# Paged sample attention: one key step per page instead of one per half page

## The chip, the core and the metric

The kernel runs on one core of one Trainium2 chip. The metric is the device time of one execution in microseconds (us). The engines of the core are TensorE (PE, whose weight loads are listed as PEld), VectorE (DVE), ScalarE (ACT), GpSimdE (POOL) and SyncE (SP, which issues nearly all DMA transfers).

## What is computed

The program is one inference step of a decoder layer for 256 prompt tokens and for 8 sequences ("batches") of 4 sample tokens each. The change concerns the attention of the sample tokens to their paged key cache of 1024 positions, 8 pages of 128 positions, 8 heads of width 128:

```python
past_k = cache_k[l][page_table].reshape(DB, past, MOBA_HEADS, MOBA_DH)
...
gate = jnp.einsum('bthd,bnhd->bthn', qq.astype(jnp.float32), kbar)   # kbar: mean key of a block of 256
...
s = (jnp.einsum('bthd,bthnkd->bthnk', qq, kg).astype(jnp.float32)
     - slopes[None, None, :, None, None] * dist.astype(jnp.float32))
p = jax.nn.softmax(s.reshape(B, qb, H, -1), axis=-1).reshape(s.shape)
return jnp.einsum('bthnk,bthnkd->bthd', p.astype(vg.dtype), vg).astype(q.dtype)
```

Each query keeps its three best past blocks of four and its own block. The kernel computes the scores of all eight pages and masks the worst block afterwards, so the keys of every page are read, transposed and multiplied with the queries.

## The kernel before, in words

Every engine has its own hand-written instruction stream. Within a stream the order is that of the program, and semaphores join the streams. Most of the kernel is large products of weights with 288 tokens: ACT rounds a weight tile into a high part (`hi`), DVE makes the remainder (`lo`), and `tile` on PE multiplies both (lines 1699, 1700, 1703). The sample attention is woven into one stage of that work: `d_batch` runs eight times, once for each batch, on each of PE, ACT and DVE.

On PE a batch of `d_batch` goes through these pieces in order:

- `tile(p_gm, b, 0, 0, 0)`, a gate tile of 48 products.
- `rows_t(b)`: two transposes that carry the previous batch's output rows into bank 5, after ACT copied them out of bank 4 (`rows_out`, semaphore `d_va`). DVE takes the result out of bank 5 in `rows_in` (line 1348) and counts `d_h`.
- The key steps, 16 half pages and a loop of 17 turns. In turn n PE makes four transposes of keys (line 1717, through `tr`) into bank 2 + n % 2, and then the four scores of the half page before (line 1713, through `one`). A score is a matmul with a stationary operand of 32 columns, and the four of a half page write to four different groups of 32 partitions of bank 6 or 7. The trace shows two records for each score.
- Between transposes and scores, a half page is copied from its bank to the buffer `KTb[n % 2]`: the even ones by ACT (line 831, called from `d_batch`, semaphore `d_kta`), the odd ones by DVE (line 1359, semaphore `d_ktd`). A copy waits for the transposes (`d_tr`) and for the scores that read the buffer last (`d_ss`).
- After the steps come the wait for `d_h`, eight scores against the batch's own keys into bank 5, and then `d_sc`, which starts the softmax on DVE.
- A second gate tile and a half tile run on PE while DVE and ACT make the softmax. Then follow the transposes of the probabilities (wait for `d_pn`), another half tile, and the products with the value pages (`PT`, line 1713).

DVE runs `rows_in` after its third key copy, while PE goes on.

The pages come in through four rings of two pages. SP issues the key pages of the next batch as the value products release the rings (`kv_read`), and the value pages as the key scores release them. The order of SP's queue is written out by hand: the next gate weights, eight value pages, the next projection weights (`pm_load`), eight key pages (line 493 issues pages, line 437 weights).

`d_P`, the score and probability rows, and `PT`, their transposes, share memory. They are used only after the key steps of a batch.

Of the kernel before, what the change touches and what calls it, by code (L numbers as in the profile page):

```python
# [14 lines left out]
P = 128  # L15
# [3 lines left out]
NS = NB * TS  # L19
NT = TP + NS  # L20
H, DH = 8, 128
# [16 lines left out]
GROUPS = P // NS  # L38
# [127 lines left out]
def build(nc, a, o):  # L166
# [24 lines left out]
    with ctx:  # L191
# [3 lines left out]
        def at(name, shape, offset, dt=F32):  # L195
            return nc.alloc_sbuf_tensor_at(name, shape, dt, offset=offset)

        def put(name, shape, dt=F32):
            off = top[0]
            n = 4 * int(np.prod(shape[1:]))  # L200
            top[0] = off + (n + 31) // 32 * 32
            assert top[0] <= nc.sbuf_usable_end, (name, top[0])
            return at(name, shape, off, dt)
# [83 lines left out]
        dmn, dmx, dsum = put("d_min", [P, 1]), put("d_max", [P, 1]), put("d_sum", [P, 1])  # L287
        dp_at = top[0]
        DP = put("d_P", [P, PAST + NS])
        PT = at("d_PT", [P, PAGES, P], dp_at)  # L290
        PTown = put("d_PT_own", [NS, P])
        hrow = put("d_hrow", [P, 2 * P])
# [123 lines left out]
        def ring(r):  # L416

            return raw[1 + r // 2][:, (r % 2) * 2 * H * DH:(r % 2 + 1) * 2 * H * DH]
# [214 lines left out]
        def _(act):  # L633
# [184 lines left out]
            mo_body(4, False, True)  # L818


            def k_copies(kts, tr_sem, ss_sem, mine, base, i, parity, copy, between=None):

                for n in range(parity, 16, 2):
                    act.wait_ge(tr_sem, i * 16 + (base + n + 1))
                    act.wait_ge(ss_sem, i * 16 + (base + n + 1))
                    copy(kts[n % 2][:], B[2 + n % 4][:].rearrange("p (h c) -> p h c", c=P)).then_inc(mine, 1)
                    if n == 4 and between:
                        between()

            def a_copy(dst, src):  # L830
                return nc.scalar.activation(dst, src, ACT.Copy)  # L831
# [14 lines left out]
            def d_batch(b, first):  # L846
                for j in range(2):
                    hi(p_gm, b, 0, j, src256(p_gm.slot(0), j))
                if not first:
                    rows_out(b)  # L850
                for n in range(0, 16, 2):
                    act.wait_ge(d_tr, b * 16 + (n + 1))
                    act.wait_ge(d_ss, b * 16 + (n + 1))
                    a_copy(KTb[0][:], B[2][:].rearrange("p (h c) -> p h c", c=P)).then_inc(d_kta, 1)
                gate_evac(p_gm, b, 0)
                pm_hi(b, 0)
                act.wait_ge(d_sm, b + 1)
                nc.scalar.activation(DP[:], DP[:], ACT.Exp, bias=dmx[:], accum_out=dsum[:]).then_inc(d_p, 1)
                gate_evac(p_gm, b, 1)
                pm_hi(b, 1)  # L860
                act.wait_ge(d_ptr, b + 1)
                a_copy(PTown[:], B[4][0:NS, 2 * P:3 * P])
                for q in range(2):
                    last = a_copy(PT[:, 4 * q:4 * q + 4, :], B[2 + q][:].rearrange("p (n c) -> p n c", c=P))
                last.then_inc(d_ptc, 1)
# [84 lines left out]
                    last = nc.scalar.activation(xP[:, h, r, :], xP[:, h, r, :], ACT.Exp, bias=xmx[:, h, r:r + 1], accum_out=xsm[:, h, r:r + 1])  # L950
            last.then_inc(c_step, 1)

            k_copies(xKT, d_tr, d_ss, d_kta, 128, 0, 0, a_copy)
            act.wait_ge(c_step, c_ptr)
            for h in range(XH):
                last = a_copy(xPT[:, h, :], B[2 + h][:])
# [84 lines left out]
        def _(dve):  # L1041
# [281 lines left out]
            dc.end(4)  # L1323


            def k_copies(kts, tr_sem, ss_sem, mine, base, i):
                for n in range(1, 16, 2):
                    dve.wait_ge(tr_sem, i * 16 + (base + n + 1))
                    dve.wait_ge(ss_sem, i * 16 + (base + n + 1))
                    nc.vector.tensor_copy(kts[1][:], B[2 + n % 4][:].rearrange("p (h c) -> p h c", c=P)).then_inc(mine, 1)  # L1330

            def gate_sig(ph, i, t, n):
# [13 lines left out]
            def rows_in(b):  # L1346
                dve.wait_ge(d_ht, b)
                nc.vector.tensor_copy(hsd[:, :, ds(b * TS - TS, TS)],
                                      B[5][:, 0:H * (NS + TS)].rearrange("p (h c) -> p h c", c=NS + TS)[:, :, 0:TS]).then_inc(d_h, 1)

            def d_batch(b, first):
                nc.vector.tensor_copy(qpad[:].rearrange("p (h c) -> p h c", c=NS + TS)[:, :, 0:TS],
                                      qs[:, :, ds(b * TS, TS)]).then_inc(d_q, 1)
                for j in range(2):
                    lo(p_gm, b, 0, j, src256(p_gm.slot(0), j))
                for n in range(1, 16, 2):
                    dve.wait_ge(d_tr, b * 16 + (n + 1))
                    dve.wait_ge(d_ss, b * 16 + (n + 1))
                    nc.vector.tensor_copy(KTb[1][:], B[3][:].rearrange("p (h c) -> p h c", c=P)).then_inc(d_ktd, 1)  # L1359
                    if n == 5 and not first:  # L1360
                        rows_in(b)

                dve.wait_ge(d_sc, b + 1)
                for q in range(2):
                    dc.run(nc.vector.reduce_sum(gs[:, 2 * q:2 * q + 2], B[6 + q][:].rearrange("p (n c) -> p n c", c=256), AX))
                dc.sync()
                dc.run(nc.vector.tensor_reduce(dmn[:], gs[:], AX, ALU.min))
                dc.sync()
                dc.run(nc.vector.scalar_tensor_tensor(geq[:], gs[:], dmn[:], K["rank"], ALU.is_equal, ALU.mult))
                dc.sync()  # L1370
                dc.run(nc.vector.reduce_max(dmx[:], geq[:], AX))
                dc.sync()
                dc.run(nc.vector.tensor_scalar(pen[:], geq[:], dmx[:], NEG, ALU.is_equal, ALU.mult))
                dc.sync()
                for n in range(BLOCKS):
                    dc.run(nc.vector.scalar_tensor_tensor(DP[:, n * 256:(n + 1) * 256], B[6 + n // 2][:, (n % 2) * 256:(n % 2) * 256 + 256],
                                                          pen[:, n:n + 1], dtab[:, n * 256:(n + 1) * 256], ALU.add, ALU.add))
                dc.run(nc.vector.tensor_tensor(DP[:, PAST:], B[5][:, 256:256 + NS], dtab[:, ds(b * -TS + (PAST + OWN), NS)], ALU.add))
                dc.sync()
                dc.run(nc.vector.reduce_max(dmx[:], DP[:], AX))  # L1380
                dc.sync()
                nc.vector.tensor_scalar(dmx[:], dmx[:], -1.0, None, ALU.mult).then_inc(d_sm, 1)
                pm_lo(b, 0)
                dve.wait_ge(d_p, b + 1)
                dc.run(nc.vector.reciprocal(dsum[:], dsum[:]))
                dc.sync()
                nc.vector.tensor_scalar(DP[:], DP[:], dsum[:], None, ALU.mult).then_inc(d_pn, 1)
                pm_lo(b, 1)
                gate_sig(p_gm, b, 0, 2)
                for j in range(2):  # L1390
                    dve.wait_ge(gemm_done, p_gm.conv(b, 3 + j))
                    nc.vector.tensor_tensor(U[:, ds(b * 2 + j, 1), :], G[p_gm.bank(2 + j)][:, 0:NT].unsqueeze(1), sg[:, j:j + 1, :],
                                            ALU.mult).then_inc(evac_done[p_gm.bank(2 + j)], 1)
# [127 lines left out]
            dc.sync()  # L1521
            nc.vector.tensor_scalar(xmx[:], xmx[:], -1.0, None, ALU.mult).then_inc(c_step, 1)

            k_copies(xKT, d_tr, d_ss, d_ktd, 128, 0)

            dve.wait_ge(c_step, c_p)
            dc.run(nc.vector.reciprocal(xsm[:], xsm[:]))
# [157 lines left out]
        def _(pe):  # L1685
# [29 lines left out]
            def tr(out, src):  # L1715
                n = src.shape[0]
                return nc.tensor.transpose(out, src, ident[0:n, 0:n])  # L1717
# [233 lines left out]
            def d_batch(b, first):  # L1951
# [2 lines left out]
                    rows_t(b)  # L1954
                pe.wait_ge(d_q, b + 1)

                for n in range(17):
                    if n < 16:
                        r, page = n // 4, n // 2 % 2
                        if n % 4 == 0:  # L1960
                            pe.wait_ge(kv_landed[r], b * 64 + 32)
                        for m in range(4):
                            c = page * H * DH + (4 * (n % 2) + m) * DH
                            last = tr(B[2 + n % 2][:, m * P:(m + 1) * P], ring(r)[:, c:c + DH])
                        last.then_inc(d_tr, 1)
                    if n:
                        pe.wait_ge((d_kta, d_ktd)[(n - 1) % 2], b * 8 + ((n - 1) // 2 + 1))
                        page = (n - 1) // 2
                        for m in range(4):
                            h = 4 * ((n - 1) % 2) + m  # L1970
                            last = one(B[6 + page // 4][m * NS:(m + 1) * NS, (page % 4) * P:(page % 4 + 1) * P],
                                       qpad[:, h * NS:(h + 1) * NS], KTb[(n - 1) % 2][:, m, :], start=h < GROUPS, stop=h >= GROUPS)
                            if m == 0 and n % 4 == 0:
                                last.then_inc(kv_read[n // 4 - 1], 1)
                        last.then_inc(d_ss, 1)
                pe.wait_ge(d_h, b + 1)
                for h in range(H):
# [239 lines left out]
```

## Time and profile before

| what | us |
|---|---|
| three timed runs | 2280.73, 2289.93, 2290.65 |
| their median | 2289.93 |
| the profiled execution's own time | 2281.03 |
| its span in the trace | 2279.5 |
| PE busy in the span | 2130.7 |
| DVE busy | 1206.3 |
| ACT busy | 797.3 |

PE is busy 93% of the span. Matmul records overlap each other, because matmuls are pipelined, so the start of a group of records minus the start of the next tells more than their summed durations. Times in the rows are microseconds from the start of the span, and the columns are explained where a view first appears.

### The profile page before, as it was taken

The numbers are of one execution on the slowest core, as the hardware profiler recorded it, in microseconds if no ns is written. First come the engines' busy times: TensorE is split into PE (matmuls) and PEld (weight loads), VectorE is DVE, ScalarE is ACT, GpSimd is POOL, SyncE is SP. The second block draws the span as 40 slices with busy tenths as digits, with TensorE's granted clock in tenths as the row PEclk, the third lists the DMA queues.
The fourth block names the chain that finished last, engine by engine and source line by source line (L and its number), as shares of the span: only waits on it lengthen the run. The fifth ranks groups of instructions, "written<-read, shape, count | busy, mean of one in ns | idle before, by whom it ended". The sixth has DMA issues, their size and how long they took to land.

```text
span 2279.5 us, 40609 instructions
## 1 busy us (share of the span) xinstructions
PE 2130.7 (93%) x16438; PEld 2009.2 (88%) x16438; DVE 1206.3 (53%) x1424; ACT 797.3 (35%) x1010; POOL 63.5 (3%) x85
## 2 busy tenths in 40 slices
PE   4999997998999999898899877999999999999997
PEld 4989896998778788888899756999999999999997
DVE  4354465343556465656446535666564456666444
ACT  3333332343333333323234333333333333333333
POOL 0011011010000000000000000000000000000000
PEclk7999997999999999999899988999999999999999
DMA  7145434454686876554444451454545555454543
GB/s 244 47 151 175 150 105 140 132 175 145 216 315 244 306 273 219 176 163 147 164 143 157 162 185 37 148 175 157 168 134 173 158 180 183 147 176 144 171 154 115
DMA packets 305491, 384.78 MB, mean 169 GB/s; under 512 B 6146, under 2 KB 278690, under 8 KB 304626
## 3 DMA queue, kind: packets, MB, share of 16 engines
q1 hardware_dynamic: 300530, 365.72, 48.9%
q0 software_dynamic: 4896, 18.13, 2.5%
q8 instruction: 49, 0.80, 0.2%
q14 instruction: 16, 0.13, 0.0%
HBM read 370.94 MB, written 12.88 MB: 168 GB/s over the span
## 4 chain that ended last, share of the span: by engine, by line
PE 87%; DVE 6%; ACT 3%; issue 2%; SPq 1%; DMA 1%; DVEq 0%; POOL 0%; PEldq 0%; ACTq 0%; PEld 0%; POOLq 0%
PE bank L1699 19%; PE bank L1700 19%; PE bank L1703 18%; PE bank L1713 8%; PE bank L1717 6%; PE bank L2158 4%; PE bank L2157 4%; PE bank L2162 4%; ACT w_hi L639 1%; DVE w_lo L1046 1%; PE bank L1710 1%; DVE n_tmp L1078 1%; PE bank L1939 1%; PE bank L1938 1%; PE bank L1942 1%
## 5 line engine op out<-in xcount | busy, mean ns | idle before, releaser
L1699 PE MATMUL bank<-xn_hi,w_hi 128*128 128x288 f32 x3152 | 882.8, 306 | 69.1 <-DVE xn_lo L1086 26.1
L1046 DVE TENSOR_TENSOR w_lo<-raw,w_hi 128x2048 fp32r<-128x2048 f32 (+2 forms) x289 | 605.0, 2096 | 616.7 <-ACT w_hi L639 614.0
L1700 PE MATMUL bank<-xn_lo,w_hi 128*128 128x288 f32 x3152 | 874.1, 303 | 0.0
L639 ACT ACTIVATE w_hi<-raw 128x2048 fp32r<-128x2048 f32 (+2 forms) x289 | 503.9, 1745 | 694.1 <-PE bank L1703 476.7
L1699 PEld LDWEIGHTS bank<-xn_hi,w_hi 128*128 128x128 f32 x3152 | 614.5, 195 | 83.5 <-issue 45.0
L1700 PEld LDWEIGHTS bank<-xn_lo,w_hi 128*128 128x128 f32 x3152 | 614.1, 195 | 0.1
L1703 PE MATMUL bank<-xn_hi,w_lo 128*128 128x288 f32 x3152 | 450.2, 295 | 0.0
L1703 PEld LDWEIGHTS bank<-xn_hi,w_lo 128*128 128x128 f32 x3152 | 429.5, 189 | 0.0
L2157 PE MATMUL bank<-f_hi,w_hi 128*128 128x288 f32 x704 | 191.4, 296 | 0.0
L2158 PE MATMUL bank<-f_lo,w_hi 128*128 128x288 f32 x704 | 190.8, 297 | 0.0
L2157 PEld LDWEIGHTS bank<-f_hi,w_hi 128*128 128x128 f32 x704 | 132.5, 188 | 0.1
L2158 PEld LDWEIGHTS bank<-f_lo,w_hi 128*128 128x128 f32 x704 | 132.4, 188 | 0.0
L1717 PE MATMUL bank<-consts,raw 128*128 128x128 f32 (+1 forms) x656 | 104.2, 290 | 16.8 <-DMA raw<-x_prompt_dram 13.9
L1717 PEld LDWEIGHTS bank<-consts,raw 128*128 128x128 f32 (+1 forms) x656 | 72.3, 145 | 42.9 <-issue 39.5
L1359 DVE COPY d_KT<-bank 128x512 f32<-128x512 f32 x64 | 44.3, 692 | 120.3 <-PE bank L1717 120.3
L2162 PE MATMUL bank<-f_hi,w_lo 128*128 128x288 f32 x704 | 103.2, 294 | 0.0
L2162 PEld LDWEIGHTS bank<-f_hi,w_lo 128*128 128x128 f32 x704 | 96.5, 188 | 0.0
L1579 DVE RECIPROCAL f_e<-f_e 128x288 f32<-128x288 f32 x44 | 85.9, 1953 | 1.5
L831 ACT ACTIVATE d_KT<-bank 128x512 f32<-128x512 f32 x64 | 38.2, 597 | 125.3 <-PE bank L1717 125.3
L1338 DVE RECIPROCAL x_gates<-x_gates 128x288 f32<-128x288 f32 (+1 forms) x24 | 61.3, 2554 | 0.8
L1713 PE MATMUL bank<-d_KT,d_qpad 128*32 128x128 f32 x1024 | 54.5, 285 | 5.4 <-DVE d_KT L1359 3.4
L1586 DVE TENSOR_TENSOR f_a<-f_g,bank 128x288 f32<-128x288 f32 x44 | 20.0, 454 | 59.5 <-PE bank L1703 49.8
(363 smaller groups left out, 1762.1 us busy)
## 6 DMA issues: line engine op xcount, KB each, us to landing
raw<-w_in_dram SPq DMA_DIRECT2D x44, 2048.0 KB, 9.0
raw<-w_ffn_gate_dram SPq DMA_DIRECT2D x22, 2048.0 KB, 8.1
raw<-w_ffn_up_dram SPq DMA_DIRECT2D x22, 2048.0 KB, 8.1
raw<-w_ffn_down_dram SPq DMA_DIRECT2D x32, 1408.0 KB, 6.6
raw<-cache_k_dram SPq DMA_DIRECT2D x64, 512.0 KB, 5.4
raw<-cache_v_dram SPq DMA_DIRECT2D x64, 512.0 KB, 5.3
raw<-w_out_dram SPq DMA_DIRECT2D x8, 2048.0 KB, 8.6
w_pm_raw<-w_proj_m_dram SPq DMA_DIRECT2D x8, 1024.0 KB, 5.6
```

The costliest lines, as they stand in the source:

```text
L639: nc.scalar.activation(like(wh[ph.half(c)], src), src, ACT.Copy).then_inc(hi_ready, 1)
L1046: nc.vector.tensor_tensor(like(wl[ph.half(c)], src), src, like(wh[ph.half(c)], src).bitcast(F32), ALU.subtract).then_inc(slot_read[ph.slot ...
L1338: dc.run(nc.vector.reciprocal(sg[:, t:t + n, :], sg[:, t:t + n, :]))
L1579: dc.run(nc.vector.reciprocal(fe[:, t, :], fe[:, t, :]))
L1699: mm(out, wh[half][:, k, :], rh[:, k, 0:n], start=k == 0, stop=False)
L1700: mm(out, wh[half][:, k, :], rl[:, k, 0:n], start=False, stop=False)
L1703: last = mm(out, wl[half][:, k, :], rh[:, k, 0:n], start=False, stop=k == KT - 1)
L1713: return mm(out, lhsT, rhs, start=start, stop=stop)
L1717: return nc.tensor.transpose(out, src, ident[0:n, 0:n])
L2157: mm(out, wh[half][:, k, :], fah[:, kk, :], start=kk == 0, stop=False)
L2158: mm(out, wh[half][:, k, :], fal[:, kk, :], start=False, stop=False)
L2162: last = mm(out, wl[half][:, k, :], fah[:, kk, :], start=False, stop=kk == FH - 1)
```

## The change

A key step becomes a whole page. PE makes eight transposes into a pair of banks (2 and 3, or 4 and 5, in turns) and then the eight scores of the page before. ACT copies the first bank of each pair and DVE the second, into one of two pairs of key buffers. The second pair, `KTb2`, lies on the memory of `d_P`. Every score group now waits for both copies. `rows_in` moves ahead of DVE's key copies. PE waits for `d_h` ahead of the second page's transposes, since these write to banks 4 and 5; the old wait for it, ahead of the own-key scores, stays. The score semaphore counts 8 for each batch instead of 16, and the later memory attention, which goes on counting with it, gets another base and is otherwise the same.

```diff
+        KTb2 = [at(f"d_KT2{n}", [P, 4, P], dp_at + n * 4 * 4 * P) for n in range(2)]
...
-                for n in range(0, 16, 2):
-                    act.wait_ge(d_tr, b * 16 + (n + 1))
-                    act.wait_ge(d_ss, b * 16 + (n + 1))
-                    a_copy(KTb[0][:], B[2][:].rearrange("p (h c) -> p h c", c=P)).then_inc(d_kta, 1)
+                for n in range(PAGES):
+                    act.wait_ge(d_tr, b * 16 + (2 * n + 1))
+                    act.wait_ge(d_ss, b * PAGES + (n + 1))
+                    a_copy((KTb, KTb2)[n % 2][0][:], B[2 + 2 * (n % 2)][:].rearrange("p (h c) -> p h c", c=P)).then_inc(d_kta, 1)
...
-                for n in range(1, 16, 2):
-                    dve.wait_ge(d_tr, b * 16 + (n + 1))
-                    dve.wait_ge(d_ss, b * 16 + (n + 1))
-                    nc.vector.tensor_copy(KTb[1][:], B[3][:].rearrange("p (h c) -> p h c", c=P)).then_inc(d_ktd, 1)
-                    if n == 5 and not first:
-                        rows_in(b)
+                if not first:
+                    rows_in(b)
+                for n in range(PAGES):
+                    dve.wait_ge(d_tr, b * 16 + (2 * n + 2))
+                    dve.wait_ge(d_ss, b * PAGES + (n + 1))
+                    nc.vector.tensor_copy((KTb, KTb2)[n % 2][1][:], B[3 + 2 * (n % 2)][:].rearrange("p (h c) -> p h c", c=P)).then_inc(d_ktd, 1)
...
-                for n in range(17):
-                    if n < 16:
-                        r, page = n // 4, n // 2 % 2
-                        if n % 4 == 0:
-                            pe.wait_ge(kv_landed[r], b * 64 + 32)
-                        for m in range(4):
-                            c = page * H * DH + (4 * (n % 2) + m) * DH
-                            last = tr(B[2 + n % 2][:, m * P:(m + 1) * P], ring(r)[:, c:c + DH])
-                        last.then_inc(d_tr, 1)
+                for n in range(PAGES + 1):
+                    if n == 1:
+                        pe.wait_ge(d_h, b + 1)
+                    if n < PAGES:
+                        if n % 2 == 0:
+                            pe.wait_ge(kv_landed[n // 2], b * 64 + 32)
+                        for h in range(H):
+                            c = n % 2 * H * DH + h * DH
+                            last = tr(B[2 + 2 * (n % 2) + h // 4][:, h % 4 * P:(h % 4 + 1) * P], ring(n // 2)[:, c:c + DH])
+                            if h % 4 == 3:
+                                last.then_inc(d_tr, 1)
                     if n:
-                        pe.wait_ge((d_kta, d_ktd)[(n - 1) % 2], b * 8 + ((n - 1) // 2 + 1))
-                        page = (n - 1) // 2
-                        for m in range(4):
-                            h = 4 * ((n - 1) % 2) + m
+                        page, kt = n - 1, (KTb, KTb2)[(n - 1) % 2]
+                        pe.wait_ge(d_kta, b * 8 + n)
+                        pe.wait_ge(d_ktd, b * 8 + n)
+                        for h in range(H):
+                            m = h % GROUPS
                             last = one(B[6 + page // 4][m * NS:(m + 1) * NS, (page % 4) * P:(page % 4 + 1) * P],
-                                       qpad[:, h * NS:(h + 1) * NS], KTb[(n - 1) % 2][:, m, :], start=h < GROUPS, stop=h >= GROUPS)
-                            if m == 0 and n % 4 == 0:
-                                last.then_inc(kv_read[n // 4 - 1], 1)
+                                       qpad[:, h * NS:(h + 1) * NS], kt[h // 4][:, m, :], start=h < GROUPS, stop=h >= GROUPS)
+                            if h == 0 and n % 2 == 0:
+                                last.then_inc(kv_read[n // 2 - 1], 1)
                         last.then_inc(d_ss, 1)
```

## Rows read from the trace of the kernel before

**Rows 1.** The page, part 1: busy us, share, instructions of each engine
```profile
PE 2130.7 (93%) x16438; PEld 2009.2 (88%) x16438; DVE 1206.3 (53%) x1424; ACT 797.3 (35%) x1010; POOL 63.5 (3%) x85
```

**Rows 2.** The page, part 4: shares by engine of the chain that ended last
```profile
PE 87%; DVE 6%; ACT 3%; issue 2%; SPq 1%; DMA 1%; DVEq 0%; POOL 0%; PEldq 0%; ACTq 0%; PEld 0%; POOLq 0%
```

**Rows 3.** Windows: length, busy PE, PEld, DVE, ACT, POOL, clock, DMA share, GB/s
```profile
664.20:680.13 15.93, 15.25 (x212) 9.58 (x210) 5.63 (x9) 6.03 (x10) 0.00 (x0) 1.00 1.05 385
...
698.32:704.92 6.60, 6.60 (x53) 6.60 (x50) 1.10 (x1) 0.39 (x1) 0.00 (x0) 1.00 0.87 307
```

**Rows 4.** Waits, all eight batches (580 to 905): total us, times, longest
```profile
PE bank L1713 <- DVE d_KT L1359: 3.4, 8, 0.4
...
PEld bank L1717 <- issue: 22.2, 112, 0.2
PEld bank L1713 <- DVE d_KT L1359: 13.6, 56, 0.7
PEld bank L1713 <- ACT d_KT L831: 10.4, 47, 0.5
```

**Rows 5.** PE timeline, middle of the key steps: start, us, what, records
```profile
672.56 0.65 PE L1717 MATMUL bank<-consts,raw 128*128 128x128 f32 x4
673.14 0.42 PE L1713 MATMUL bank<-d_KT,d_qpad 128*32 128x128 f32 x8
673.50 0.66 PE L1717 MATMUL bank<-consts,raw 128*128 128x128 f32 x4
```

**Rows 6.** Timeline, first key steps of the same batch: PE, ACT, DVE
```profile
664.10 0.38 PE L1717 MATMUL bank<-consts,d_hrow 128*128 128x128 f32 x2
664.32 1.04 PE L1717 MATMUL bank<-consts,raw 128*128 128x128 f32 x8
664.95 0.60 ACT L831 ACTIVATE d_KT<-bank 128x512 f32<-128x512 f32 x1 [6.83 <-PE bank L1717]
665.39 0.69 DVE L1359 COPY d_KT<-bank 128x512 f32<-128x512 f32 x1 [6.68 <-PE bank L1717]
665.60 0.43 PE L1713 MATMUL bank<-d_KT,d_qpad 128*32 128x128 f32 x8 [0.25 <-ACT d_KT L831]
...
670.09 0.18 DVE L1348 COPY d_h<-bank 128x32 f32 x1
```

**Rows 7.** Timeline, last key steps and own-key scores: PE, DVE
```profile
678.21 0.66 PE L1717 MATMUL bank<-consts,raw 128*128 128x128 f32 x4
...
678.90 0.69 DVE L1359 COPY d_KT<-bank 128x512 f32<-128x512 f32 x1 [1.19 <-PE bank L1717]
679.65 0.43 PE L1713 MATMUL bank<-d_KT,d_qpad 128*32 128x128 f32 x8 [0.43 <-DVE d_KT L1359]
679.89 0.31 PE L1713 MATMUL bank<-a_ks,d_qpad 128*32 128x32 f32 x16
```

**Rows 8.** PE timeline, the products with the value pages
```profile
694.17 3.66 PE L1713 MATMUL bank<-raw,d_PT 128*32 128x256 f32 x64
```

**Rows 9.** SP's issues of the next key pages; the last four's median landing
```profile
696.19 8.85 SPq L493 DMA_DIRECT2D raw<-cache_k_dram  x8
...
raw<-cache_k_dram SPq DMA_DIRECT2D x4, 512.0 KB, 6.2
```

**Rows 10.** Timeline after the key steps: softmax end, PE's use of it
```profile
687.33 0.77 DVE L1387 TENSOR_SCALAR d_P<-d_P,d_sum 128x1056 f32<-128x1056 f32 x1
...
689.86 1.14 PE L1717 MATMUL bank<-consts,d_P 128*128 128x128 f32 x9
```

**Rows 11.** Window in a later stage, columns as in rows 3
```profile
947.00:951.00 4.00, 4.00 (x20) 4.00 (x20) 2.71 (x3) 0.00 (x0) 0.38 (x1) 0.57 0.16 30
```

**Rows 12.** PE timeline just ahead of that window: start, us, what, [idle before]
```profile
946.74 0.40 PE L1699 MATMUL bank<-xn_hi,w_hi 128*128 128x288 f32 x1 [2.21 <-DVEq L1425]
```

**Rows 13.** Chain of waits in that window: start, us, what
```profile
947.15 0.15 PE bank L1700
947.30 0.24 PE bank L1699
```

More of the change, by code:

```diff
@@ L818, in _, with k_copies @@
             mo_body(4, False, True)
-            def k_copies(kts, tr_sem, ss_sem, mine, base, i, parity, copy, between=None):
+            def k_copies(kts, tr_sem, ss_sem, mine, base, i, parity, copy, ss_base):
                 for n in range(parity, 16, 2):
                     act.wait_ge(tr_sem, i * 16 + (base + n + 1))
-                    act.wait_ge(ss_sem, i * 16 + (base + n + 1))
+                    act.wait_ge(ss_sem, i * 16 + (ss_base + n + 1))
                     copy(kts[n % 2][:], B[2 + n % 4][:].rearrange("p (h c) -> p h c", c=P)).then_inc(mine, 1)
-                    if n == 4 and between:
-                        between()
             def a_copy(dst, src):
@@ L951, in _ @@
             last.then_inc(c_step, 1)
-            k_copies(xKT, d_tr, d_ss, d_kta, 128, 0, 0, a_copy)
+            k_copies(xKT, d_tr, d_ss, d_kta, 128, 0, 0, a_copy, 64)
             act.wait_ge(c_step, c_ptr)
@@ L1323, in _, with k_copies @@
             dc.end(4)
-            def k_copies(kts, tr_sem, ss_sem, mine, base, i):
+            def k_copies(kts, tr_sem, ss_sem, mine, base, i, ss_base):
                 for n in range(1, 16, 2):
                     dve.wait_ge(tr_sem, i * 16 + (base + n + 1))
-                    dve.wait_ge(ss_sem, i * 16 + (base + n + 1))
+                    dve.wait_ge(ss_sem, i * 16 + (ss_base + n + 1))
                     nc.vector.tensor_copy(kts[1][:], B[2 + n % 4][:].rearrange("p (h c) -> p h c", c=P)).then_inc(mine, 1)
@@ L1522, in _ @@
             nc.vector.tensor_scalar(xmx[:], xmx[:], -1.0, None, ALU.mult).then_inc(c_step, 1)
-            k_copies(xKT, d_tr, d_ss, d_ktd, 128, 0)
+            k_copies(xKT, d_tr, d_ss, d_ktd, 128, 0, ss_base=64)
             dve.wait_ge(c_step, c_p)
```

## The prediction

> **What bounds the kernel now.** First the page. PE is busy 93% of the span [rows 1], and the chain of work that ended last runs through PE for 87% of it [rows 2]. So time is won where PE wins it, and only if what comes next does not wait for somebody else. Next, the stretch that is changed. The windows over one batch show the key steps from 664.20 to 680.13, 15.93 us, with PE at the full clock (1.00) while ACT and DVE are each busy some 6 us of them; the same point of the next batch lies at 704.92, so a batch takes 40.72 us [rows 3]. Third, the waits. In all eight batches together PE itself waits only a few us for key copies, but its weight loads show two small gaps at every step: 0.2 us "issue" ahead of transposes, 112 times, and 0.2 to 0.3 us ahead of scores, put down to the copies [rows 4]. Last, the timeline, which tells what the gaps cost: transposes start at 672.56, scores at 673.14, the next transposes at 673.50 [rows 5]. A step takes 0.94 us.
>
> What part of that 0.94 is work? Two transposes in a row span 0.38 us and eight, the first two half pages, 1.04, so one more costs (1.04 − 0.38)/6 = 0.11 [rows 6], and four take 0.44. Four scores followed by matmuls of the same shape take 679.89 − 679.65 = 0.24 [rows 7]. Work is therefore 0.68, and 0.26 is lost at the two changes between transposes and scores: 0.58 − 0.44 = 0.14 on the way in, and 0.36 − 0.24 = 0.12 on the way out [rows 5]. I read the loss as the cost of changing the array between whole (128x128) and four column strips (128x32), for two reasons. On the way out nothing is waited for in most turns, and the gap is there all the same. From key scores to own-key scores a wait stands too, but the shape stays, and there is no gap [rows 7]. The Trainium skill says the same (TensorEngine Tiling, Key Properties: a change of the tiling mode drains TensorE), which would make the loss one per change, and this trace agrees with 0.12 and 0.14 us.
>
> **The steps, part by part.** *Fewer changes.* A page now costs two steps, 1.88 us. After it costs 8 × 0.11 = 0.88 for transposes, 0.46 for scores, and one pair of changes, 0.26: 1.60. The scores are 0.24 for the first four and 0.22 for the second four; the second figure is from the value products, where 16 groups of four matmuls over 256 columns take (3.66 − 0.38)/15 = 0.22, so 0.11 for 128 columns, with two such passes to four scores [rows 8]. A page saves 0.28.
>
> *Both copies ahead of the scores.* In the middle this wait should be covered. The last copy of a page ends 0.69 + 4 × 0.11 + 0.69 = 1.82 us after its transposes began: the present last half page starts its copy 0.69 after its first transpose, and the copy takes 0.69 [rows 7]. Scores see it 0.05 later, at 1.87. They are due one page step (1.60) and the next page's transposes (about 1.0) after that beginning, at 2.6. The cover is 0.7 us, and it would hold even if a copy took twice as long. Behind the waiting scores on PE are the rest of the key steps and the gate tile; DVE and ACT have nothing else to do meanwhile.
>
> *The two ends of the key steps.* Count from the first transpose, now 664.32. Before, the own-key scores come at 679.89, which is 15.57 [rows 6, 7]. After: two pages of transposes, 16 × 0.11 = 1.76, and the change, 0.09, give 1.85 for the first scores; the DVE copy that they need ends at 666.08 [rows 6], seen at 1.81, so it is just in time. (The 0.14 on the way in holds about 0.05 that only a transpose group behind scores pays.) The third page starts at 1.85 + 0.46 + 0.12 = 2.43, the eighth at 2.43 + 5 × 1.60 = 10.43. Its scores wait for its DVE copy until 10.43 + 1.87 = 12.30, and nothing covers that wait: PE has done the seventh page's scores by 11.9 and idles 0.4, about what it idles there now (0.43) [rows 7]. Own-key scores at 12.30 + 0.46 = 12.76. The gain is 15.57 − 12.76 = 2.81 us a batch.
>
> *`rows_in` earlier, and the wait for `d_h`.* The row transposes start at 664.10 and end at 664.48; DVE is idle then (6.68 us ahead of its first copy), and the copy takes 0.18 [rows 6], so `d_h` is counted at about 664.75. The second page's transposes are due at 664.32 + 0.88 = 665.20. Behind this wait stands all of PE, but it is covered by 0.4 us: nothing. On DVE nothing is late, since the first key copy waits until 665.39 anyhow.
>
> *The pages.* The key pages do not come earlier, but are wanted earlier. The next batch's eight are issued within 8.85 us from 696.19, and the last four land 6.2 us after issue [rows 9]; the last one, issued near 704.7, thus lands near 710.9. Counted from that batch's first transpose (664.32 + 40.72 = 705.04) this is 5.9, and the seventh page's transposes, which need that ring, will start at 2.43 + 4 × 1.60 = 8.83. The second ring's last page is the fourth issue, near 700, and lands near 706.2, at 1.2; it is needed at 2.43. The covers are 2.9 and 1.2 us. Behind the keys come 2 MB of gate weights and 4 MB of value pages, at 385 GB/s [rows 3] some 16 us, so the last values are there by about 22; SP gets their last release at 12.3. PE wants them now at 694.17 − 664.32 = 29.9 [rows 8] and then at 27. That is covered too.
>
> *What is late next.* The softmax starts from the own-key scores and ends at 688.10; PE wants it at 689.86, 1.8 us later [rows 10]. Both move together, so nothing changes. After the eighth batch the loads follow PE's own progress.
>
> **The sum.** 8 batches × 2.81 = 22.5 us. The profiled execution took 2281.03 (span 2279.5), which gives 2258.5. That execution and one of the three timed ones lie near 2281, the other two near 2290, so the median stands 8.9 above the profile, and the same saving from it gives 2267.4. I cannot tell from one trace on which side a median of new runs falls, and take the middle, 2263.
>
> **Bounds of what the trace does not show.** Scores behind two waits instead of one: the nearest row is the 0.05 us from the end of a copy to the scores that waited for it [rows 7], so 0 to 0.05 a page, 0 to 0.4 a batch; I take 0. The second four scores: 0.22 to 0.24, so up to 0.16 a batch. Copies of ACT and DVE side by side in time: they overlap by 0.16 us at the first step and show their usual 0.60 and 0.69 [rows 6]; if they took twice as long, only the uncovered last one would show, 0.7 a batch. On the other side, the waits view puts the gap ahead of the scores down to copies. If that is right, 0.09 of each page's gap goes too, 0.7 a batch. So a batch gains between 2.81 − 0.4 − 0.16 − 0.7 = 1.55 and 3.5: 12 to 28 us in all.
>
> **Rivals.** *The loss belongs to the matmuls, not to the change of shape*: each four transposes and four scores would cost 0.94 in any order. For it: the profile names no cause on the way out, only "issue" [rows 4]. Against it: eight transposes in a row, and key scores followed by own-key scores, run without the gap [rows 6, 7]. Six pages would lose the 0.28 each, 1.7 a batch, and the gain would be 1.1 a batch, 9 us: 2272 to 2281.
>
> *The pages come too late*: a ring's pages land behind the transposes that want them. DMA works at 385 GB/s, its full share, throughout the key steps [rows 3], which speaks for it; the covers of 1.2 and 2.9 us speak against it. Each us of lateness beyond the cover costs 1 us a batch; if the landings slip by 2.2 us, 8 us of the gain go: about 2271.
>
> *Slower: the clock falls in the key steps.* In a later stage PE waited 2.21 us [rows 12], and soon after it the granted clock is 0.57 over 4 us [rows 11]; products of 288 columns then come every 0.24 us instead of every 0.15 [rows 13], at the lower of the two levels, 1.2 GHz. Transposes make up 0.44 of 0.94 us of a step now and 0.88 of 1.60 after, 16 of them in a row at the beginning. If the clock fell to half in the key steps of every batch, their work (8 × 1.34 = 10.7 us) would take 0.24/0.15 = 1.6 times as long, 6.4 us more a batch against 2.8 gained: 8 × 3.6 = 29 us slower than before, 2281 + 29 = 2310 at least. It decides from the point where 2.8/6.4 = 44% of the key steps run at the lower level. Against it: the clock is 1.00 in these stretches [rows 3], with transposes for half of the work, and PE idles less after than before. The Trainium skill speaks for it (TensorE: Matmul & The Clock Gate, Part 4: transposes do not count as busy in the same way); no run here shows this so far.
>
> **How the numbers follow.** Forecast 0.83, the loss belonging to the matmuls 0.07, late pages 0.04, clock 0.04, the rest 0.02 for a change that does nothing because another wait takes all of it. The range takes in the gains of 12 to 28 us and both levels of the runs: 2281 − 28 = 2253 to 2290 − 12 = 2278. A difference below 0.5%, 11.4 us, can hardly be told from none in this kernel. Faster by more: 0.87, from the forecast and most of the late pages. Within: 0.09, the first rival and the rest. Slower: 0.04, the clock.
>
> **What would show it.** In the new trace, transposes should start every 1.60 us, with eight in one group and 16 score records in the next. The own-key scores should come 12.8 us after the first transpose, and the batch should repeat every 37.9. The only idle PE time should be about 0.4 us ahead of the eighth page's scores, put down to DVE's copy. A page step of 1.88 would mean that the loss belongs to the matmuls; a gap ahead of transposes released by a DMA, late pages; a clock below 1.00 in these windows, the third rival. A gain far from 2.8 a batch with these steps in place would mean that another stage took it back.

## The result and the profile after

| | before | after |
|---|---|---|
| median of the timed runs, us | 2287.1 (2280.73 to 2290.65) | 2267.93 (2265.13 to 2271.87) |
| profiled execution, us | 2281.03 | 2271.87 |
| key steps: first transpose to own-key scores, us | 15.57 | 13.07 |
| one batch to the next, us | 40.72 | 38.23 |

The changed kernel takes 0.9918 of the time of before (95% interval 0.9891 to 0.9944), 19 us less by the medians. A second comparison gave 0.9915 (0.9893 to 0.9937). The forecast was 2263.

The page first: PE is as busy as before by share, with the same number of PE instructions [rows 1].

```profile
span 2270.3 us, 40673 instructions
...
PE 2118.1 (93%) x16438; PEld 2018.1 (89%) x16438; DVE 1207.0 (53%) x1424; ACT 797.4 (35%) x1010; POOL 63.5 (3%) x85
```

The windows over the key steps of one batch and over the gate work after them (columns as in rows 3). They show the granted clock at 1.00 throughout. The first window ends where the own-key scores begin, that of [rows 3] where they are over, so the two lengths are not to be compared:

```profile
631.70:644.91 13.21, 12.72 (x196) 10.07 (x198) 5.73 (x9) 5.90 (x10) 0.00 (x0) 1.00 1.05 371
644.91:654.90 9.99, 9.99 (x96) 9.95 (x88) 8.84 (x18) 2.64 (x5) 0.00 (x0) 1.00 0.82 325
```

The PE timeline of the same batch, with the first transposes of the next one in the last line. The batch repeats after 670.07 − 631.84 = 38.23:

```profile
631.84 1.91 PE L1716 MATMUL bank<-consts,raw 128*128 128x128 f32 x16
633.85 0.65 PE L1712 MATMUL bank<-d_KT,d_qpad 128*32 128x128 f32 x16
634.43 1.09 PE L1716 MATMUL bank<-consts,raw 128*128 128x128 f32 x8
635.45 0.64 PE L1712 MATMUL bank<-d_KT,d_qpad 128*32 128x128 f32 x16
636.03 1.09 PE L1716 MATMUL bank<-consts,raw 128*128 128x128 f32 x8
...
670.07 1.91 PE L1716 MATMUL bank<-consts,raw 128*128 128x128 f32 x16
```

From one group of eight transposes to the next it is 636.03 − 634.43 = 1.60 us, as worked out; two half pages took 1.88 [rows 5]. The end of the key steps, in the timeline of all engines:

```profile
642.42 1.09 PE L1716 MATMUL bank<-consts,raw 128*128 128x128 f32 x8
...
643.64 0.69 DVE L1360 COPY d_KT<-bank 128x512 f32<-128x512 f32 x1 [0.91 <-PE bank L1716]
...
644.44 0.41 PEld L1712 LDWEIGHTS bank<-d_KT,d_qpad 128*32 128x32 f32 x16 [0.63 <-ACT d_KT L830]
644.47 0.64 PE L1712 MATMUL bank<-d_KT,d_qpad 128*32 128x128 f32 x16 [0.39 <-DVE d_KT L1360]
...
644.91 0.34 PE L1712 MATMUL bank<-a_ks,d_qpad 128*32 128x32 f32 x16
```

PE idles 0.39 us ahead of the last page's scores, put down to DVE's copy, as forecast. From the first batch's key steps to the end of the eighth batch that is PE's only wait. The gap of 0.2 us "issue" ahead of its weight loads for transposes, 112 times before [rows 4], is there 48 times, six in each batch:

```profile
PE bank L1712 <- DVE d_KT L1360: 3.0, 8, 0.4
...
PEld bank L1716 <- issue: 9.5, 48, 0.2
```

But two distances are longer than worked out. The first scores come 633.85 − 631.84 = 2.01 us after the first transpose, not 1.85. From the eighth page's first transpose to its scores it is 644.47 − 642.42 = 2.05, not 1.87.

A third thing stands out, outside the change. The key steps of the first batch begin at 582.92 in the profile of before and at 593.84 in that of after, and all instructions ahead of them are the same in both kernels. So the two profiled spans differ by 9 us only, while the eight batches gain 8 × 2.49 = 19.9. The PE timeline at the first batch, of before and then of after, with after's own-key scores of that batch:

```profile
582.92 1.03 PE L1717 MATMUL bank<-consts,raw 128*128 128x128 f32 x8
```
```profile
593.84 1.91 PE L1716 MATMUL bank<-consts,raw 128*128 128x128 f32 x16
...
606.71 0.34 PE L1712 MATMUL bank<-a_ks,d_qpad 128*32 128x32 f32 x16
```

### The profile page after: what moved, and what is told of

It reads as the page before. It is cut to its first block, busy times and chain, and to the rows that moved or that the text cites. A ratio compares the mean times of both kernels' runs of the same rounds, so it can differ in the third digit from the quotient of the medians.

```text
span 2270.3 us, 40673 instructions
## 1 busy us (share of the span) xinstructions
PE 2118.1 (93%) x16438; PEld 2018.1 (89%) x16438; DVE 1207.0 (53%) x1424; ACT 797.4 (35%) x1010; POOL 63.5 (3%) x85
## 4 chain that ended last, share of the span: by engine, by line
PE 87%; DVE 6%; issue 2%; ACT 2%; SPq 1%; DMA 1%; DVEq 0%; POOL 0%; PEldq 0%; ACTq 0%; PEld 0%; POOLq 0%
PE bank L1698 19%; PE bank L1699 19%; PE bank L1702 18%; PE bank L1712 8%; PE bank L1716 5%; PE bank L2160 4%; PE bank L2159 4%; PE bank L2164 4%; ACT w_hi L640 1%; PE bank L1709 1%; DVE w_lo L1045 1%; DVE n_tmp L1077 1%; PE bank L1938 1%; PE bank L1937 1%; PE bank L1941 1%
## 5 line engine op out<-in xcount | busy, mean ns | idle before, releaser
L1716 PE MATMUL bank<-consts,raw 128*128 128x128 f32 (+1 forms) x656 | 89.1, 282 | 16.2 <-DMA raw<-x_prompt_dram 13.3
L834 ACT ACTIVATE x_gates<-bank 128x288 f32<-128x288 f32 x32 | 12.9, 404 | 95.7 <-PE bank L1702 95.7
```

## Experiments

Three questions were open. Was the 0.26 us a step really the price of changing the array's shape? Where do the 0.3 us a batch go that were forecast and not found? And are the 11 us ahead of the first batch made by the change? All figures from experiments below are stage times within one profiled execution, except where a median is named. The ends of the key steps are read in the second batch, the middle of them in the third.

**Half pages in turns again, with the new buffers.** The order within the loop goes back to four transposes, four scores; the bank pairs, the key buffers and the waits of the copies stay as changed. Each four scores wait for their own copy alone.

```diff
-                        for h in range(H):
+                    for q in range(2):
+                        for h in range(4 * q, 4 * q + 4):
 ...
-                        pe.wait_ge(d_kta, b * 8 + n)
-                        pe.wait_ge(d_ktd, b * 8 + n)
+                        pe.wait_ge((d_kta, d_ktd)[q], b * 8 + n)
```

> The changed kernel with its bank pairs, buffers and waits, but four transposes and four scores in turns again, so 16 changes of shape a batch instead of 8. From the first transpose of a batch to its own-key scores it took 15.57 us before and 13.07 after. Theory (each change between 128x128 and 128x32 costs 0.12 to 0.14 us): a half-page step of 0.94 us again and about 14.9 us for the stretch; most of the gain is gone though every copy is done long ahead. Rival (the gap ahead of scores was a wait for the copies): a half-page step of 0.80 to 0.85 us, about 13.3 us.

```profile
669.18 0.66 PE L1716 MATMUL bank<-consts,raw 128*128 128x128 f32 x4
669.77 0.43 PE L1712 MATMUL bank<-d_KT,d_qpad 128*32 128x128 f32 x8
670.12 0.66 PE L1716 MATMUL bank<-consts,raw 128*128 128x128 f32 x4
```

The PE timeline in the middle of the key steps: 0.94 us a half page, with 0.59 on the way in and 0.35 on the way out, though these copies end about 1 us ahead of their scores. The stretch is 638.55 − 623.72 = 14.83 us. The copies did not make the gap; the number of changes does. The run with the split wait, further down, differs from this one in the order of transposes and scores alone, and its stretch is 12.61 us: the order by itself is worth 2.22 us a batch.

```profile
623.72 1.47 PE L1716 MATMUL bank<-consts,raw 128*128 128x128 f32 x12
...
638.55 0.31 PE L1712 MATMUL bank<-a_ks,d_qpad 128*32 128x32 f32 x16
```

**Scores in the shape of the transposes.** In the kernel before, each score takes 128 query columns and writes all 128 partitions, so the scores of neighbouring heads are added together and the sample attention is another one.

```diff
-    last = one(B[6 + page // 4][m * NS:(m + 1) * NS, ...], qpad[:, h * NS:(h + 1) * NS], ...
+    last = one(B[6 + page // 4][:, ...], qpad[:, min(h * NS, 160):min(h * NS, 160) + P], ...
```

> The kernel before, but every score takes 128 query columns instead of 32, so that transposes and scores have the same 128x128 shape; the scores of neighbouring heads are added together, so the sample attention computed is another one. Eight score records in a row at 0.11 us are 0.88, four transposes 0.44. Theory (the loss is the change of shape): a half-page step of 1.32 us, with no gap ahead of transposes. Rival (the loss comes with each alternation between transposes and scores, whatever their shape): 1.32 + 0.26 = 1.58 us.

```profile
690.72 1.06 PE L1713 MATMUL bank<-d_KT,d_qpad 128*128 128x128 f32 x8
691.61 0.60 PE L1717 MATMUL bank<-consts,raw 128*128 128x128 f32 x4
692.05 1.06 PE L1713 MATMUL bank<-d_KT,d_qpad 128*128 128x128 f32 x8
...
692.83 0.47 PEld L1717 LDWEIGHTS bank<-consts,raw 128*128 128x128 f32 x4
```

A half page takes 692.05 − 690.72 = 1.33 us: 0.89 for eight score records, 0.44 for four transposes, no more. The weight loads of the transposes (last row) carry no idle time ahead of them, where every such row of the kernel before had 0.20 of "issue" [rows 4]. Transposes and scores still alternate as before, so it is not the alternation: with one shape there is no loss.

**The second wait behind the first four scores.**

```diff
-                        pe.wait_ge(d_kta, b * 8 + n)
-                        pe.wait_ge(d_ktd, b * 8 + n)
                         for h in range(H):
+                            if h % 4 == 0:
+                                pe.wait_ge((d_kta, d_ktd)[h // 4], b * 8 + n)
```

> The changed kernel, but the wait for DVE's copy stands between the fourth and the fifth score of a page, so each score group has one wait ahead of it. Theory (the second wait ahead of the first score is a separate instruction that costs 0.1 us where nothing covers it, and the last page's scores wait in full for the later copy): the first scores come at 1.9 instead of 2.01 us after the first transpose, the own-key scores at 12.65 instead of 13.07: 3.4 us in all. Rival (a second wait costs nothing): the first scores stay at 2.01, only the last page's first four scores move ahead, own-key scores at 12.85.

```profile
627.53 1.91 PE L1716 MATMUL bank<-consts,raw 128*128 128x128 f32 x16
629.37 0.65 PE L1712 MATMUL bank<-d_KT,d_qpad 128*32 128x128 f32 x16
...
639.15 0.69 DVE L1360 COPY d_KT<-bank 128x512 f32<-128x512 f32 x1 [0.91 <-PE bank L1716]
...
639.90 0.16 PEld L1712 LDWEIGHTS bank<-d_KT,d_qpad 128*32 128x32 f32 x8 [0.35 <-DVE d_KT L1360]
...
640.14 0.31 PE L1712 MATMUL bank<-a_ks,d_qpad 128*32 128x32 f32 x16
```

First scores at 629.37 − 627.53 = 1.84, the 1.85 of the forecast's sum. Own-key scores at 640.14 − 627.53 = 12.61. The first four scores of a page no longer wait for DVE's copy at all, so how far they moved is not the price of the second wait, though the text above takes it for that. The price is read where a score waits for DVE's copy in both kernels. DVE's last copy runs from 639.15 to 639.84 here, and the scores that need it are loaded at 639.90, 0.06 later; in the changed kernel it was 644.47 − 644.33 = 0.14. That is 0.08 us for the second wait. In the changed kernel the list of instructions of line 1970, PE's wait for `d_ktd`, shows the cause:

```profile
L1970 PEldq EVENT_SEMAPHORE  x64: 51/51/51, 595.6 to 873.8; - x64
```

One wait rides on the weight load of the first score. The second becomes an instruction of its own, and of the two it is DVE's wait, the later one, that went there. With the wait split, the list of PE's wait line has no such instruction. This is also why the profile of the changed kernel puts the idle weight loads at 644.44 down to ACT, whose wait stayed on the instruction, and the idle matmuls at 644.47 down to DVE: the second reading is the right one.

**The order of the two waits ahead of a key copy.**

```diff
-                    dve.wait_ge(d_tr, b * 16 + (2 * n + 2))
                     dve.wait_ge(d_ss, b * PAGES + (n + 1))
+                    dve.wait_ge(d_tr, b * 16 + (2 * n + 2))
```

The same in ACT's stream.

> The changed kernel, with the two waits ahead of each key copy in the other order, the one that ends last (for the transposes) second. Theory (with thresholds that differ, a register operation stands between the two waits, and it falls behind the later one: 0.09 us on every copy): DVE's last copy starts 0.04 instead of 0.12 us after the last transpose's end, first scores at 1.92, own-key scores at 12.89 us: 1.4 us in all. Rival (the later start has another cause): 2.01 and 13.07 as they were.

```profile
621.49 1.91 PE L1716 MATMUL bank<-consts,raw 128*128 128x128 f32 x16
623.40 0.64 PE L1712 MATMUL bank<-d_KT,d_qpad 128*32 128x128 f32 x16
...
631.96 1.09 PE L1716 MATMUL bank<-consts,raw 128*128 128x128 f32 x8
...
633.09 0.69 DVE L1360 COPY d_KT<-bank 128x512 f32<-128x512 f32 x1 [0.91 <-PE bank L1716]
...
634.36 0.33 PE L1712 MATMUL bank<-a_ks,d_qpad 128*32 128x32 f32 x15
```

DVE's last copy starts 633.09 − 631.96 = 1.13 us after the page's first transpose, the 1.13 of the forecast's sum; in the changed kernel 643.64 − 642.42 = 1.22. First scores at 1.91 and own-key scores at 12.87. In the kernel before, both waits had the same threshold. In the changed one they count to 16 and to 8 a batch, and the list of instructions of DVE's second wait line shows 49 register operations of 0.04 us, seven in each batch from the second on (ahead of a batch's first copy stands a fused one):

```profile
L1359 DVEq ALU_OP  x49: 40/40/40, 633.8 to 873.0; - x49
```

With the transposes' wait first, that operation falls behind the wait that ends last. Turning the order round put it ahead. The same list for the last copy of the batch alone shows it, of the changed kernel (the copy starts at 643.64) and then of this run (633.09):

```profile
L1359 DVEq ALU_OP  x1: 40/40/40, 643.6 to 643.6; - x1
```
```profile
L1359 DVEq ALU_OP  x1: 40/40/40, 632.1 to 632.1; - x1
```

**Both, and the engines swapped.** Each page's first half goes to DVE (0.69 us a copy) and its second half to ACT (0.60), with the split wait and the turned order.

```diff
-    a_copy((KTb, KTb2)[n % 2][0][:], B[2 + 2 * (n % 2)][:] ...
+    a_copy((KTb, KTb2)[n % 2][1][:], B[3 + 2 * (n % 2)][:] ...
-    nc.vector.tensor_copy((KTb, KTb2)[n % 2][1][:], B[3 + 2 * (n % 2)][:] ...
+    nc.vector.tensor_copy((KTb, KTb2)[n % 2][0][:], B[2 + 2 * (n % 2)][:] ...
```

> The changed kernel with the split wait, the wait order of the copies turned round, and the engines swapped: DVE (0.69 us a copy) takes the first half of a page and ACT (0.60) the second. Theory: first scores 1.84 us and own-key scores 12.45 us after the first transpose (13.07 in the changed kernel, 12.61 with the split wait alone), so 8 x 0.62 = 5.0 us less than the changed kernel and 25.0 us less than before. Rival (ACT now has its last copy later and delays the gate work and so the softmax): the stretch shrinks, but the batch's period stays at 37.77 us or grows.

```profile
621.47 1.91 PE L1716 MATMUL bank<-consts,raw 128*128 128x128 f32 x16
623.31 0.64 PE L1712 MATMUL bank<-d_KT,d_qpad 128*32 128x128 f32 x16
...
633.89 0.31 PE L1712 MATMUL bank<-a_ks,d_qpad 128*32 128x32 f32 x16
...
658.99 1.91 PE L1716 MATMUL bank<-consts,raw 128*128 128x128 f32 x16
```

First scores at 1.84, own-key scores at 12.42, a batch in 658.99 − 621.47 = 37.52 us. No run has the swap alone, so its own share is not shown. What follows the key steps takes 25.1 us; it was 25.2 before (40.72 − 15.57) and after (38.23 − 13.07), so ACT's later copy delays nothing. The timed median is 2261.49 (2257.86 to 2265.78) against 2287.34 of before in the same comparison, a ratio of 0.9886 (0.9865 to 0.9908). This is the fastest kernel of the study: 5.5 us below the changed kernel's 2267.04 beside it, with 8 × 0.71 = 5.7 worked out from the periods. The intervals of the two ratios overlap, so it is the periods that carry this difference.

**The rows' copy and its wait alone.** The kernel before, with `rows_in` ahead of DVE's key copies, and PE waiting for `d_h` ahead of the third half page, where bank 2 is used for the second time.

```diff
-                    if n == 5 and not first:
-                        rows_in(b)
+                if not first:
+                    rows_in(b)
 ...
+                    if n == 2:
+                        pe.wait_ge(d_h, b + 1)
```

> The kernel before with one part of the change alone: the copy of the output rows ahead of DVE's key copies, and PE's wait for it ahead of the third half page. Theory (covered by some 0.4 us): stretch of 15.57 us and period of 40.72 us as before. Rival (PE waits for DVE there, or DVE's first key copy gets late): a stretch of 15.7 us or more.

```profile
629.54 1.04 PE L1717 MATMUL bank<-consts,raw 128*128 128x128 f32 x8
...
629.86 0.19 DVE L1348 COPY d_h<-bank 128x32 f32 x1 [6.13 <-PE bank L1717]
...
645.12 0.31 PE L1713 MATMUL bank<-a_ks,d_qpad 128*32 128x32 f32 x16
...
670.26 1.04 PE L1717 MATMUL bank<-consts,raw 128*128 128x128 f32 x8
```

Stretch 645.12 − 629.54 = 15.58, period 40.72: it costs nothing. The copy is over 0.5 us after the first transpose.

**The same two kernels once more**, the changed one and the one before, for where the first batch begins.

> The changed kernel again, with its profile. Theory (its first batch came 10.9 us later than that of the kernel before by chance of the execution, in code that is the same): the stretch and the period are again 13.07 and 38.23 us, while the first transpose of the first batch may lie anywhere between 582 and 594 us; the timed median lies 20 us below that of before. Rival (the change itself makes the stages ahead of it slower): the first batch again at 590 us or later, and a gain nearer to 10 us.

> The kernel before again, with its profile. Theory: stretch 15.57 and period 40.72 us again; the first batch need not begin at 582.9 us again. Rival (that kernel always gets there by 583): within 1 us of 582.9.

The first transposes of the first batch, changed kernel, then kernel before:

```profile
587.10 1.91 PE L1716 MATMUL bank<-consts,raw 128*128 128x128 f32 x16
```
```profile
588.54 1.04 PE L1717 MATMUL bank<-consts,raw 128*128 128x128 f32 x8
```

The kernel before came to its first batch at 582.92 in one execution and at 588.54 in the other, the changed one at 593.84 and 587.10. Stretch and period were the same in both executions of each kernel, 15.57 and 40.72, and 13.07 and 38.23. So the eight batches repeat to a few hundredths, and the 583 to 594 us ahead of them vary by up to 11 us between executions of the same code. The change does not make that difference; what does is not known. The timed median of this comparison, 2267.04 against 2287.34, gives 20.3 us, next to 8 × 2.49 = 19.9 from the periods.

## Why the forecast was right, and where its sizes were off

**The loss at each change: right, shown.** 0.12 and 0.14 us at a change between 128x128 and 128x32 was worked out from rows of the kernel before. Two runs bear it out from opposite sides: with the old number of changes and the new buffers the 0.94 came back, and with one shape in the old order the loss was gone. The page step of 1.60 us came out to the hundredth. The first rival, that the loss belongs to the matmuls, falls. So does the reading of the waits view that put the gap ahead of scores down to copies.

**Two waits ahead of the scores: the term that was mis-sized.** The prediction bounded this at 0 to 0.05 us a page and took 0. Where nothing covers it, it costs 0.08: the later of the two waits became an instruction of its own. The bound came from the delay of a single wait, which was no near row for a second one. In the six middle pages it is covered, as the step of 1.60 shows, but it shows at both ends of a batch's key steps.

**The copy's start: a term that was left out.** The sum let DVE's copy start as soon after the transposes as before. The new thresholds put a register operation behind the wait, 0.09 us. With the second wait this makes 0.17 at each end; 0.16 was measured at the first scores and 0.18 at the last, so 2.81 − 0.34 = 2.47 a batch, against 2.49 from the periods; the stretch fell from 15.57 to 13.07 and the period by the same. Over eight batches, 22.5 became 19.9.

**The starting point.** The middle between 2281 and 2290 was taken, 2285.5. More runs put the median of before at 2287.1. With the 2.6 us of gain that were missing, 0.7 of other variation is left to the measured 2267.93.

**The covers: right.** `d_h` costs nothing, shown by the run with that part alone. Late pages did not occur: no wait of PE for a DMA stands in this stage. The copies side by side in time show their usual 0.60 and 0.69. The softmax moves with the key steps; the 25.2 us after them are unchanged.

**The clock: the rival that would have made it slower did not occur.** The key steps have the granted clock at 1.00 with transposes for more than half of their PE time, and PE works without a wait of its own until the 0.39 us at the end. What the Trainium skill states in TensorE: Matmul & The Clock Gate, Part 4, that transposes do not count as busy in the same way, changed nothing here: in groups of eight or sixteen, between scores and full tiles, they left the clock at its upper level, 2.4 GHz. The price of this rival was too low: the prediction took 0.15 us for a product of 288 columns at the upper level, one step of a chain around the point where the level fell [rows 13]. In the same stage of the kernel before, with the granted clock at 1.00 again, products start at 950.63, 950.76 and 950.90, every 0.13 us. The lower level would cost 0.24/0.13 = 1.8 times, not 1.6.

## What to carry to other kernels

Count the changes of shape on TensorE: each between full and column-strip matmuls cost 0.12 to 0.14 us here whatever was waiting, so group by shape as far as banks and buffers allow. When groups get larger, price the ends separately, where copies are uncovered: the split wait, the wait order and the swap of engines together won back 0.7 us a batch. And compare two profiles stage by stage from a common mark: the spans differed by 9 us and the changed stage by 20, because the stages ahead of it had varied by 11.

## What the runs showed of the hardware that was not expected

- Of two waits ahead of a matmul, one became a separate instruction on PE's sequencer (64 of them, 0.05 us each). From the end of the copy to the scores it was 0.14 us instead of 0.06.
- Two thresholds that differ put a register operation of 0.04 us between two waits; with the later wait first, the copy started 0.09 us later. The first batch has constant thresholds and no such operation; its stretch in the changed kernel is 606.71 − 593.84 = 12.87 us, that of the run with the waits turned round.
- A value page took 6.9 us from issue to landing (median) in the changed kernel and 5.3 in the kernel before, by part 6 of the two pages (before first). Nothing waited for them. Why they took longer is not shown; the same pages are asked for within a shorter batch.

```profile
raw<-cache_v_dram SPq DMA_DIRECT2D x64, 512.0 KB, 5.3
```
```profile
raw<-cache_v_dram SPq DMA_DIRECT2D x64, 512.0 KB, 6.9
```
